# Three up projections of a fused two-block network as seven half-size products in place of eight

## The chip, the core and the metric

The kernel runs on one core of a Trainium2 chip, as one program. The metric is the device time of a run in microseconds. Its engines: TensorE (PE, matmuls; PEld is its weight load), VectorE (DVE), ScalarE (ACT), GpSimd (POOL) and SyncE (SP, which issues the weight loads).

## The reference, cut to what matters

The network has two blocks of two layers each on 512 tokens of width 1024; the first carries 256 context tokens too. All arithmetic is float32. The change lies in the feed-forwards of the second block, four in number (two in each of two layers):

```python
def rmsnorm_2(x, g, eps=EPS):
    return x * lax.rsqrt(jnp.mean(x * x, axis=-1, keepdims=True) + eps) * g

def swiglu(h, w_gate, w_up, w_down):
    return (jax.nn.silu(h @ w_gate) * (h @ w_up)) @ w_down

# second_block, layer 0 (recurrent) and 1 (attention)
x = x + 0.5 * swiglu(rmsnorm_2(x, ffn1_norm[layer]), ffn1_w_gate[layer], ffn1_w_up[layer], ffn1_w_down[layer])
h = rmsnorm_2(x, mix_norm[layer]); x = x + mixer(h)
x = x + 0.5 * swiglu(rmsnorm_2(x, ffn2_norm[layer]), ffn2_w_gate[layer], ffn2_w_up[layer], ffn2_w_down[layer])
```

The weights `w_gate` and `w_up` are 1024 x 2816, `w_down` is 2816 x 1024. So the product `h @ [w_gate, w_up]` is 512 x 1024 by 1024 x 5632.

## The kernel before, in words

Tokens lie along the free axis, width along the 128 partitions: `k.X` holds 8 tiles of 128 x 512. The width of 2816 is 22 tiles (`FT`). Each float32 operand is split into a high part (rounded to fp32r) and a low part, and a product is three matmuls, high x high, high x low, low x high (`dense`, L673 to L675).

The weights come as one stream, in the order of `split_plan`. For each chunk (128 x 1024 floats, one weight tile for all 8 width tiles): SP loads it into a ring of three raw slots, ACT writes its high part (`split_hi`, L288), DVE its low part (`split_lo`, L297), and PE uses it. There are three pairs of high and low. The split of chunk c + 2 stands in each engine's program at the step of chunk c. Each engine works through its own program in order; semaphores join them.

A feed-forward (`gated_ffn`) takes tile j of gate and of value, 24 matmuls each. DVE multiplies the gate by the root of the norm (L1304), ACT takes the SiLU (L1275), POOL multiplies by the root once more for the value (L1288), DVE multiplies by the value (L1308), and ACT and DVE split the hidden tile (L1278, L1311). The 22 tiles are cut into three groups of 8, 8 and 6; behind each group stand 8 down products over its tiles, each added to `k.X` by DVE (L1318). One tile more than the group needs is made ahead of the down products. During the last eight of them, `Feed` makes the input of what follows: ACT scales each tile of X by the gain (L903) and squares it (L906), DVE makes the low part (L914), and POOL sums the squares (L923). The root itself (L944, L949) is taken behind the first tile of the next stage. Two stages, `recurrent` and `diff_attention`, end in `ProjectOut`, which calls the same `Feed`.

The stages of the second block in order are s_up10, the recurrent mixer, s_up20, keys and values, s_up11, the attention, s_up21.

## Time and profile before

| | |
|---|---|
| Time of the runs | 3851.02, 3855.47, 3858.65 us, median 3855.47 |
| Span of the profiled execution | 3857.1 us, between the second and the third of these |
| PE busy | 3750.6 us, 97% |
| DVE, ACT, POOL busy | 51%, 35%, 10% |
| Mean granted clock of TensorE | 0.977 of 2.4 GHz |
| DMA | 330 MB, 86 GB/s |

The span is the time from the first to the last instruction of one execution; no time of that execution is given apart from it. A busy PE is not a PE at its peak, since matmuls overlap: the distance of their starts tells more than their durations. The durations of the other engines count the time in which an instruction stands still on the engine after its semaphores are there.

### The profile page before, as it was taken

How to read it: one execution, taken by the hardware profiler on the slowest of the kernel's cores; microseconds unless marked ns; L12 is line 12 of the kernel's file. 1: busy time of each engine (PE TensorE's matmuls, PEld its weight loads, DVE VectorE, ACT ScalarE, POOL GpSimd, SP SyncE). 2: the span in 40 equal slices, each digit the busy share in tenths (PEclk: the TensorE clock that was granted, in tenths of full speed). 3: DMA queues.
4: the chain of work that ended last, by engine and by line, in shares of the span. 5: the costliest groups of instructions: out<-in, count | busy, mean ns of one | idle time of the engine just before them, and what ended most of it. 6: DMA issues, size and time to landing. Idle time of an engine off the chain costs nothing.

```text
span 3857.1 us, 44920 instructions
## 1 busy us (share of the span) xinstructions
PE 3750.6 (97%) x18180; PEld 3048.8 (79%) x18180; DVE 1964.6 (51%) x3059; ACT 1334.7 (35%) x2194; POOL 390.9 (10%) x296
## 2 busy tenths in 40 slices
PE   7999999999999998999999999999999999979999
PEld 4868778888888866788888886888877888658888
DVE  5446566755546355544443457534453344574443
ACT  3245443323234334323332236322242222473222
POOL 0000002850000010000010011101020001101000
PEclk8899999999999989999999999999999999999999
DMA  5200012343322201233233332333222333203332
GB/s 214 91 28 1 1 50 81 131 134 120 121 92 76 61 28 34 87 98 98 93 99 93 98 99 82 92 97 96 93 88 88 99 98 93 67 19 97 96 97 93
DMA packets 105821, 329.99 MB, mean 86 GB/s; under 512 B 11536, under 2 KB 13200, under 8 KB 105616
## 3 DMA queue, kind: packets, MB, share of 16 engines
q1 hardware_dynamic: 103024, 320.38, 26.1%
q10 hardware_dynamic: 2592, 6.74, 0.5%
q8 instruction: 144, 2.36, 0.3%
q14 instruction: 61, 0.50, 0.0%
HBM read 324.99 MB, written 2.10 MB: 85 GB/s over the span
## 4 chain that ended last, share of the span: by engine, by line
PE 88%; DVE 3%; ACT 1%; issue 1%; POOL 0%; ACTq 0%; DVEq 0%
PE ps L673 23%; PE ps L674 23%; PE ps L675 23%; PE ps L1544 2%; PE ps L1529 1%; PE ps L1519 1%; PE ps L1520 1%; PE ps L1424 1%; PE ps L1426 1%; PE ps L1425 1%; PE ps L2637 1%; PE ps L2635 1%; PE ps L2601 1%; DVE t L3396 1%; PE ps L1516 0%
## 5 line engine op out<-in xcount | busy, mean ns | idle before, releaser
L673 PE MATMUL ps<-t 128*128 128x512 f32 (+1 forms) x4480 | 1689.0, 377 | 12.4 <-DVE t L297 9.0
L674 PE MATMUL ps<-t 128*128 128x512 f32 (+1 forms) x4480 | 1675.5, 374 | 0.0
L675 PE MATMUL ps<-t 128*128 128x512 f32 (+1 forms) x4480 | 1674.1, 374 | 0.0
L673 PEld LDWEIGHTS ps<-t 128*128 128x128 f32 x4480 | 848.9, 189 | 173.0 <-DVE t L297 10.8
L674 PEld LDWEIGHTS ps<-t 128*128 128x128 f32 x4480 | 848.9, 189 | 152.9 <-issue 5.9
L675 PEld LDWEIGHTS ps<-t 128*128 128x128 f32 x4480 | 848.3, 189 | 149.9
L297 DVE TENSOR_TENSOR t<-t 128x1024 fp32r<-128x1024 f32 (+1 forms) x517 | 645.9, 1249 | 442.4 <-ACT t L288 439.1
L288 ACT ACTIVATE t<-t 128x1024 fp32r<-128x1024 f32 (+1 forms) x517 | 533.2, 1031 | 780.0 <-PE ps L675 674.2
L1288 POOL TENSOR_TENSOR t<-t 128x512 f32<-128x512 f32 x88 | 113.8, 1293 | 1218.2 <-ACT t L1275 1218.2
L1318 DVE SCALAR_TENSOR_TENSOR t<-ps,t 128x512 f32<-128x512 f32 x96 | 66.4, 692 | 236.3 <-PE ps L675 236.3
L1278 ACT ACTIVATE t<-t 128x512 fp32r<-128x512 f32 x88 | 55.6, 632 | 340.3 <-DVE t L1308 340.3
L1275 ACT ACTIVATE t<-t 128x512 f32<-128x512 f32 x88 | 55.6, 632 | 334.9 <-DVE t L1304 334.9
L923 POOL TENSOR_TENSOR t<-t 128x512 f32<-128x512 f32 x42 | 71.0, 1690 | 769.4 <-ACT t L906 769.4
L592 DVE SCALAR_TENSOR_TENSOR t<-t 128x512 f32<-128x512 f32 x168 | 137.1, 834 | 13.6 <-DMA t<-w_ada 6.0
L1304 DVE TENSOR_TENSOR t<-ps,t 128x512 f32<-128x512 f32 x88 | 60.9, 692 | 160.5 <-PE ps L675 160.4
L1308 DVE TENSOR_TENSOR t<-ps,t 128x512 f32<-128x512 f32 x88 | 60.8, 691 | 144.8 <-PE ps L675 144.8
L1162 DVE SCALAR_TENSOR_TENSOR t<-ps,t 128x512 f32<-128x512 f32 x72 | 47.6, 662 | 127.5 <-PE ps L675 127.5
L1544 PE MATMUL ps<-t 128*128 128x64 f32 x896 | 110.7, 269 | 0.1
L1544 PEld LDWEIGHTS ps<-t 128*128 128x128 f32 x896 | 107.6, 192 | 0.2 <-ACT t L1562 0.2
L1097 ACT ACTIVATE t<-ps,t 128x512 f32<-128x512 f32 x66 | 46.1, 705 | 155.9 <-PE ps L675 149.3
L1131 DVE SCALAR_TENSOR_TENSOR t<-ps,t 128x511 f32<-128x511 f32 x66 | 43.5, 659 | 103.3 <-ACT t L1097 103.3
L1311 DVE TENSOR_TENSOR t<-t 128x512 fp32r<-128x512 f32 x88 | 61.0, 693 | 61.4 <-ACT t L1278 61.4
(381 smaller groups left out, 3461.9 us busy)
## 6 DMA issues: line engine op xcount, KB each, us to landing
t<-w_s_up SPq DMA_DIRECT2D x176, 512.0 KB, 3.6
t<-w_up SPq DMA_DIRECT2D x88, 512.0 KB, 3.7
t<-w_ada SPq DMA_DIRECT2D x160, 256.0 KB, 3.0
t<-w_s_down SPq DMA_DIRECT2D x64, 512.0 KB, 3.6
t<-w_down SPq DMA_DIRECT2D x32, 512.0 KB, 3.7
t<-w_s_down SPq DMA_DIRECT2D x32, 384.0 KB, 3.0
t<-w_ada SPq DMA_DIRECT2D x16, 512.0 KB, 10.6
t<-w_rec_in SPq DMA_DIRECT2D x16, 512.0 KB, 3.7
```

Of the source, the lines that this page charges most:

```text
L288: k.A.activation(self.hi[:, o, 0:f], self.raw[:, s, 0:f], ACT.Copy).then_inc(self.hi_done.sem, 1)
L297: k.V.tensor_tensor(self.lo[:, o, 0:f], self.raw[:, s, 0:f], self.hi[:, o, 0:f].bitcast(F32), ALU.subtract).then_inc(self.lo_done.sem, 1)
L592: ins = k.V.scalar_tensor_tensor(out=acc, in0=self.slot(h), scalar=by, in1=acc, op0=ALU.mult, op1=ALU.add)
L673: k.T.matmul(out, wh, hh, start=(i == 0), stop=False)
L674: k.T.matmul(out, wh, hl, start=False, stop=False)
L675: ins = k.T.matmul(out, wl, hh, start=False, stop=(i == len(kts) - 1))
L923: k.G.tensor_tensor(self.ACC, k.TMP[:, 0, :] if m == 1 else self.ACC, k.TMP[:, m % 2, :], ALU.add)\
L1288: k.G.tensor_tensor(a, a, RS, ALU.mult).then_inc(sm.sem, 1)
L1304: k.V.tensor_tensor(a, gate_bank[j], RS, ALU.mult).then_inc(ga.sem, 1)
L1311: k.V.tensor_tensor(lo, a, hi.bitcast(F32), ALU.subtract).then_inc(hl.sem, 1)
L1318: k.V.scalar_tensor_tensor(out=k.X[:, j, :], in0=down_bank[i], scalar=0.5, in1=k.X[:, j, :], op0=ALU.mult, op1=ALU.add).then_inc(res.sem, 1)
L1544: ins = k.T.matmul(b[:, 0:v.shape[1]], self.o(i)[:, c * 128:(c + 1) * 128], v, start=(c == 0), stop=(c == nb - 1))
```

## The change

In s_up10, s_up20 and s_up21 the up projection is done by Winograd's form of Strassen's scheme; s_up11 stays. A unit u is two tiles of gate and two of value. Its weights are four quarters: A11, A12 the gate (even and odd width tiles), A21, A22 the value. The input is cut by the parity of the width tile and by halves of the tokens, 256 each. Seven products take the place of eight: A11, S1 = A21 + A22, S2 = S1 - A11, A12, S3 = A22 - S2, S4 = A12 - S2, A22, each with one of seven blocks of the input, of which three (T2, T3, T4) and T1 are sums as well. A product is 2 x 4 x 3 = 24 matmuls of 256 columns into one of three PSUM banks.

POOL makes the four weight sums of a unit in place in the raw slots (`Stream.sum`), and all seven operands are split by ACT and DVE as chunks were. In these stages there are six raw slots and four pairs; the split stands three chunks ahead (`look`), and SP looks nine ahead. A quarter comes as two DMAs in rows of 512 bytes. `seven_ffn` puts the halves together: ACT keeps three products out of PSUM, DVE adds the later ones to them and scales, POOL scales the other two. `BlockFeed` makes the seven blocks in place of `Feed`; the recurrent and key stages have some tiles at fixed places.

```diff
...
```diff
+    def seven(up, down):
+        at = 0
+        for g, (a, b) in enumerate(GROUPS):
+            upto = min(b // 2 + 1, FT // 2)
+            order.extend((up, (u, part)) for u in range(at, upto) for part in PARTS)
+            at = upto
+            order.extend((down, 8 * g + m) for m in range(8))
...
-    feed("s_up10", "s_down10")
+    seven("s_up10", "s_down10")
...
+                if part == "A11":
+                    unit = {q: load(name, 4 * u + QUARTERS.index(q)) for q in ("A11", "A21", "A22", "A12")}
+                    self.sums[name, u] = {p: (n + PARTS.index(p), unit[q][0], unit[q][1]) for p, q in (
+                        ("A11", "A11"), ("S1", "A21"), ("S2", "A11"), ("A12", "A12"), ("S3", "A21"), ("S4", "A12"),
+                        ("A22", "A22"))}
...
+                if part in ("S3", "S4", "A22"):
+                    raw_free[x] = n
+                if part == "S4":
+                    raw_free[self.sums[name, u]["S2"][1]] = n
...
+            tiles = self.k.weights[name].rearrange("(u f g p j e n) -> u g e f p j n", f=2, g=2, p=P, j=4, e=2, n=128)
+            return [tiles[u, q // 2, q % 2, f] for f in range(2)]
...
+    def load(self, a):
         k = self.k
+        name, i, x, before, stage = self.loads[a]
+        if before >= 0:
+            if before == int(before):
+                k.sp.wait_ge(self.lo_done.at(before + 1))
+            else:
+                for t in self.opened[stage]:
+                    k.sp.wait_ge(t)
+        f = CHUNKS[name][i]
+        if name in SEVEN:
+            for h, tile in enumerate(self.source(name, i)):
+                to = self.slot(x)[:, 512 * h:512 * h + 512].rearrange("p (j n) -> p j n", j=4)
+                k.S.dma_start(to, tile).then_inc(self.landed[x].sem, 16)
+            return
...
+    def look(self, c):
+
+        for a, b in ((self.begin[x], self.finish[x]) for x in SEVEN):
+            if c < a <= c + 2:
+                return a
+            if a <= c < b:
+                return max(min(c + 3, b - 1), c + 2)
+        return c + 2
...
+
+        k, at = self.k, self.sums[name, u]
+        slot = {p: self.slot(x) for p, (n, x, t) in at.items()}
+        split = {p: self.lo_done.at(n + 1) for p, (n, x, t) in at.items()}
+        if part == "S1":
+            k.pool.wait_ge(at["S1"][2])
+            k.pool.wait_ge(at["A22"][2])
+            k.G.tensor_tensor(slot["S1"], slot["S1"], slot["A22"], ALU.add).then_inc(self.made.sem, 1)
+        elif part == "S2":
+            k.pool.wait_ge(self.made_at(name, u, "S1"))
+            k.pool.wait_ge(split["A11"])
+            k.G.tensor_tensor(slot["S2"], slot["S1"], slot["A11"], ALU.subtract).then_inc(self.made.sem, 1)
+        elif part == "S3":
+            k.pool.wait_ge(self.made_at(name, u, "S2"))
+            k.pool.wait_ge(split["S1"])
+            k.G.tensor_tensor(slot["S3"], slot["A22"], slot["S2"], ALU.subtract).then_inc(self.made.sem, 1)
+        else:
+            k.pool.wait_ge(self.made_at(name, u, "S2"))
+            k.pool.wait_ge(split["A12"])
+            k.G.tensor_tensor(slot["S4"], slot["A12"], slot["S2"], ALU.subtract).then_inc(self.made.sem, 1)
...
+class BlockFeed:
...
+    def act_hi(self, p, part):
+        k, o = self.k, self.SPANS[part]
+        if part == 0:
+            k.act.wait_ge(self.at("beside", 4 * p + 1))
+        elif part == 1:
+            k.act.wait_ge(self.at("scaled", 2 * p + 2))
+        else:
+            k.act.wait_ge(self.at("beside", 4 * p + 4) if p < 3 else self.at("late", 3))
+        k.A.activation(self.blocks.hi[:, p, o], self.Y[:, 256 + o.start:256 + o.stop], ACT.Copy).then_inc(self.sem["hi"], 1)
+
+    def act(self, m, free=()):
+        k, (p, odd) = self.k, divmod(m, 2)
+        for t in free:
+            k.act.wait_ge(t)
+        if m == 7:
+            k.stream.split_hi(self.first + 1)
+        k.act.wait_ge(self.finished(m, 0))
+        k.act.wait_ge(self.at("beside", 4 * p))
+        k.act.wait_ge(self.at("lo", 3 * p - 1 if odd else 3 * p - 2))
+        k.A.activation(self.Y[:, self.O if odd else self.E], k.X[:, m, :], ACT.Copy, scale=self.gain(m))\
+            .then_inc(self.sem["scaled"], 1)
+        if odd:
+            self.act_hi(p, 1)
+            if m == 7:
+                self.act_hi(p, 2)
+            self.act_square(m)
+        else:
+            if p:
+                self.act_hi(p - 1, 2)
+            self.act_square(m)
+            self.act_hi(p, 0)
...
+    def pool(self):
+        k, Y = self.k, self.Y
+        for p in range(4):
+            k.pool.wait_ge(self.at("scaled", 2 * p + 1))
+            k.pool.wait_ge(self.at("lo", 3 * p - 2))
+            k.pool.wait_ge(self.at("beside", 4 * p))
+            k.G.tensor_tensor(Y[:, self.T1], Y[:, 0:256], Y[:, 256:512], ALU.subtract).then_inc(self.sem["beside"], 1)
+            if p == 3:
+                k.stream.sum(self.up, 0, "S1")
+                k.stream.sum(self.up, 0, "S2")
+            self.pool_add(2 * p)
+            if p < 3:
+                k.pool.wait_ge(self.at("scaled", 2 * p + 2))
+                k.pool.wait_ge(self.at("lo", 3 * p))
+                k.pool.wait_ge(self.at("beside", 4 * p + 1))
+                k.G.tensor_tensor(Y[:, self.T2], Y[:, 768:1024], Y[:, self.T1], ALU.subtract).then_inc(self.sem["beside"], 1)
+                k.G.tensor_tensor(Y[:, self.T3], Y[:, 768:1024], Y[:, 0:256], ALU.subtract).then_inc(self.sem["beside"], 1)
+                k.pool.wait_ge(self.at("beside", 4 * p + 2))
+                k.G.tensor_tensor(Y[:, self.T4], Y[:, 1024:1280], Y[:, self.T2], ALU.subtract).then_inc(self.sem["beside"], 1)
+            self.pool_add(2 * p + 1)
...
+def seven_ffn(k, up, down, following=None):
...
+        def pe_unit(u, c):
+            for q in range(7):
+                w = st.operand(c + q, up, (u, PARTS[q]), 8)
+                if q == 0:
+                    x_bank[u], before = k.banks.take(ev.at(7 * u + 6))
+                elif q == 1:
+                    y_bank[u], before = k.banks.take(ev.at(7 * u + 4))
+                elif q == 3:
+                    z_bank[u], before = k.banks.take(ev.at(7 * u + 1))
+                elif q == 2:
+                    before = sn.at(3 * u + 1)
+                elif q == 4:
+                    before = sn.at(3 * u + 3)
+                elif q == 5:
+                    before = sn.at(3 * u + 2)
+                else:
+                    before = ev.at(7 * u + 3)
+                k.pe.wait_ge(before)
+                bank = (x_bank, y_bank, x_bank, z_bank, x_bank, y_bank, x_bank)[q][u]
+                for f in range(2):
+                    out = bank[:, 256 * f:256 * f + 256]
+                    for p in range(4):
+                        if u == 0:
+                            k.pe.wait_ge(source.ready(p, blocks[q]))
+                        bh, bl = (t[:, p, 256 * blocks[q]:256 * blocks[q] + 256] for t in (source.blocks.hi, source.blocks.lo))
+                        wh, wl = w.k(4 * f + p)
+                        k.T.matmul(out, wh, bh, start=(q in (0, 1, 3) and f == 0 and p == 0), stop=False, skip_group_check=True)
+                        k.T.matmul(out, wh, bl, start=False, stop=False, skip_group_check=True)
+                        ins = k.T.matmul(out, wl, bh, start=False, stop=(p == 3), skip_group_check=True)
+                ins.then_inc(pd.sem, 1)
+                st.used[c + q] = pd.at(7 * u + q + 1)
+                if u == 0 and q == 2:
+                    source.pe_sum()
...
+        def act_keep(u, q):
+
+            src, slot = ((x_bank, 1), (y_bank, 2), (x_bank, 0))[q]
+            k.act.wait_ge(hl.at(u - 1))
+            k.act.wait_ge(pd.at(7 * u + q + 1))
+            k.A.activation(UT[:, u % 2, slot, :], src[u], ACT.Copy).then_inc(sn.sem, 1)
+
+        def act_silu(u, h):
+            a = UT[:, u % 2, h, :]
+            k.act.wait_ge(ev.at(7 * u + (2 if h else 5)))
+            k.A.activation(a, a, ACT.Silu).then_inc(si_.sem, 1)
+
+        def act_hidden(u):
+            k.act.wait_ge(dd.at(8 * ((2 * u - HID) // 8) + 8) if 2 * u >= HID else None)
+            k.act.wait_ge(ev.at(7 * u + 7))
+            k.A.activation(hidden(hid.hi, u), UT[:, u % 2, 0:2, :].rearrange("p h (f t) -> p h f t", f=2), ACT.Copy)\
+                .then_inc(hh.sem, 1)
...
+                if kind == "up":
+                    for q in range(7):
+                        st.split_hi(st.look(c + q))
+                        if q == 0 and left is not None:
+                            act_hidden(left)
+                        if q < 3:
+                            act_keep(j, q)
+                        if j == 0 and q == 3:
+                            source.act_root()
+                        if q == 4:
+                            act_silu(j, 1)
+                        if q == 6:
+                            act_silu(j, 0)
+                    left = j
...
+        def pool_scale(u, h):
+
+            slot = 1 if h else 2
+            a = halves(UT[:, u % 2, slot, :])
+            if h:
+                k.pool.wait_ge(si_.at(2 * u + 1))
+            else:
+                k.pool.wait_ge(ev.at(7 * u + 3))
+            k.pool.wait_ge(source.rstd())
+            k.G.tensor_tensor(a, a, factor(h), ALU.mult).then_inc(rm.sem, 1)
+
+        def pool_program():
+            last = {9 // 2: 0, 17 // 2: 0, 10: 0}
+            for u in range(n_units):
+                if u in (0, 5, 9):
+                    if u:
+                        st.sum(up, u, "S1")
+                        st.sum(up, u, "S2")
+                st.sum(up, u, "S3")
+                st.sum(up, u, "S4")
+                near = u not in (4, 8, 10)
+                if near:
+                    st.sum(up, u + 1, "S1")
+                pool_scale(u, 1)
+                if near:
+                    st.sum(up, u + 1, "S2")
+                pool_scale(u, 0)
...
+        def dve_even(u, q):
+
+            t2, t1, b2 = (UT[:, u % 2, x, :] for x in range(3))
+            k.dve.wait_ge(pd.at(7 * u + q + 1))
+            if q == 3:
+                k.dve.wait_ge(sn.at(3 * u + 1))
+                k.V.tensor_tensor(t1, t1, z_bank[u], ALU.add).then_inc(ev.sem, 1)
+                k.dve.wait_ge(ev.at(7 * u + 1))
+                k.V.tensor_tensor(halves(t1), halves(t1), factor(1), ALU.mult).then_inc(ev.sem, 1)
+            elif q == 4:
+                k.dve.wait_ge(sn.at(3 * u + 2))
+                k.V.tensor_tensor(b2, b2, x_bank[u], ALU.add).then_inc(ev.sem, 1)
+            elif q == 5:
+                k.dve.wait_ge(sn.at(3 * u + 3))
+                k.V.tensor_tensor(t2, t2, y_bank[u], ALU.add).then_inc(ev.sem, 1)
+                k.dve.wait_ge(ev.at(7 * u + 4))
+                k.V.tensor_tensor(halves(t2), halves(t2), factor(0), ALU.mult).then_inc(ev.sem, 1)
+            else:
+                k.dve.wait_ge(rm.at(2 * u + 1))
+                k.V.tensor_tensor(t1, x_bank[u], t1, ALU.mult).then_inc(ev.sem, 1)
+                k.dve.wait_ge(rm.at(2 * u + 2))
+                k.dve.wait_ge(si_.at(2 * u + 2))
+                k.V.tensor_tensor(t2, t2, b2, ALU.mult).then_inc(ev.sem, 1)
+
+        def dve_hidden(u):
+            k.dve.wait_ge(hh.at(u + 1))
+            k.V.tensor_tensor(hidden(hid.lo, u), UT[:, u % 2, 0:2, :].rearrange("p h (f t) -> p h f t", f=2),
+                              hidden(hid.hi, u).bitcast(F32), ALU.subtract).then_inc(hl.sem, 1)
...
+                if kind == "up":
+                    for q in range(7):
+                        st.split_lo(st.look(c + q))
+                        if q == 0 and left is not None:
+                            dve_hidden(left)
+                        if j == 0 and q == 3:
+                            source.dve_rstd()
+                            k.dve.wait_ge(source.rstd())
+                        if q > 2:
+                            dve_even(j, q)
+                    left = j
...
-            while ahead <= min(what[1] + 2, len(st.plan) - 1):
+            while ahead < st.need[min(what[1] + (2 if what[1] < st.first_look - 3 else 9), len(st.plan) - 1)]:
...
-        half_ffn(k, "s_up10", "s_down10", following=following("mix_norm_2"))
-        recurrent(k, following("ffn2_norm_2"))
+        modulated_ffn(k, "up1", "down1", 1, False, HA, following=seven("ffn1_norm_2", "s_up10"))
+        for name in ("norm_", "gather_"):
+            k.retire(name)
+        seven_ffn(k, "s_up10", "s_down10", following=following("mix_norm_2"))
```
```

POOL's program in the first changed stage, before: the sums of squares (L923) and the 22 multiplications by the root (L1288), and what stands around them (L2699 in the first block's mixer, L2937 in the recurrent one).

```order
L2699 TENSOR_TENSOR t<-t 128x128 x40
L923 TENSOR_TENSOR t<-t 128x512 x7
L1288 TENSOR_TENSOR t<-t 128x512 x22
L923 TENSOR_TENSOR t<-t 128x512 x7
L2937 TENSOR_TENSOR t<-t 128x512 x8
```

The same engine after, from the second unit of s_up10 on. L436, L440, L444 and L448 make S1, S2, S3 and S4, L1783 scales; `raw_more` are the three slots more.

```order
L1783 TENSOR_TENSOR t<-t 128x512
L440 TENSOR_TENSOR raw_more_49<-raw_more_49 128x1024
L1783 TENSOR_TENSOR t<-t 128x512
L444 TENSOR_TENSOR raw_more_49<-t,raw_more_49 128x1024
L448 TENSOR_TENSOR raw_more_49<-raw_more_49 128x1024
L436 TENSOR_TENSOR t<-t,raw_more_49 128x1024
L1783 TENSOR_TENSOR t<-t 128x512
L440 TENSOR_TENSOR t<-t 128x1024
```

A row of POOL's between two SiLUs has become a queue in which the scaling (L1783) stands behind the next unit's S1, and the next S3 behind both scalings.

DVE before, for one tile: the splits (L297), the gate (L1304), the value (L1308) and the hidden tile's low part (L1311).

```order
L1304 TENSOR_TENSOR t<-ps,t 128x512
L297 TENSOR_TENSOR t<-t 128x1024
L1308 TENSOR_TENSOR t<-ps,t 128x512
L1311 TENSOR_TENSOR t<-t 128x512
L297 TENSOR_TENSOR t<-t 128x1024
```

DVE after, for one unit, from the split of A12 to the last but one step. L421 is the split, L1830 the hidden tile of the unit before, L1810 to L1826 put the products together; the rows with `ps` read PSUM.

```order
L421 TENSOR_TENSOR t<-t 128x1024
L1830 TENSOR_TENSOR t<-t 128x2x2x256
L421 TENSOR_TENSOR t<-t 128x1024
L421 TENSOR_TENSOR lo_more_51<-t,hi_more_50 128x1024
L421 TENSOR_TENSOR t<-raw_more_49,t 128x1024
L1810 TENSOR_TENSOR t<-t,ps 128x512
L1812 TENSOR_TENSOR t<-t 128x512
L421 TENSOR_TENSOR t<-raw_more_49,t 128x1024
L1815 TENSOR_TENSOR t<-t,ps 128x512
L421 TENSOR_TENSOR t<-t 128x1024
L1818 TENSOR_TENSOR t<-t,ps 128x512
L1820 TENSOR_TENSOR t<-t 128x512
```

The split of S2, L1823 and L1826 follow. For two tiles DVE had four splits and six operations of 512 columns; now it has seven splits, one of 1024 for the hidden tiles and seven of 512.

## Rows read from the trace of the kernel before

**Rows 1.** The page: section 1, and the chain that ended last (section 4)
```profile
span 3857.1 us, 44920 instructions
...
PE 3750.6 (97%) x18180; PEld 3048.8 (79%) x18180; DVE 1964.6 (51%) x3059; ACT 1334.7 (35%) x2194; POOL 390.9 (10%) x296
...
PE 88%; DVE 3%; ACT 1%; issue 1%; POOL 0%; ACTq 0%; DVEq 0%
PE ps L673 23%; PE ps L674 23%; PE ps L675 23%; PE ps L1544 2%; PE ps L1529 1%; PE ps L1519 1%; PE ps L1520 1%; PE ps L1424 1%; PE ps L1426 1%; PE ps L1425 1%; PE ps L2637 1%; PE ps L2635 1%; PE ps L2601 1%; DVE t L3396 1%; PE ps L1516 0%
```

**Rows 2.** 100 us of s_up10: busy us of each engine (x instructions), clock, DMA
```profile
2000.00:2100.00 100.00, 100.00 (x443) 82.81 (x442) 39.58 (x43) 24.31 (x28) 6.46 (x5) 1.00 0.32 96
```

**Rows 3.** Timeline of PE where the width changes: start us, us, line, form
```profile
805.13 0.28 PE L673 MATMUL ps<-t 128*128 128x256 f32 x1
...
807.89 0.28 PE L675 MATMUL ps<-t 128*128 128x256 f32 x1
808.01 0.40 PE L673 MATMUL ps<-t 128*128 128x512 f32 x1
```

**Rows 4.** Single lines: count, duration in ns as min/median/max, forms
```profile
L297 DVE TENSOR_TENSOR t<-t x517: 953/1226/1733, 52.6 to 3843.0; 128x1024 fp32r<-128x1024 f32 x156, 128x768 fp32r<-128x768 f32 x17
...
L288 ACT ACTIVATE t<-t x517: 829/1044/1101, 46.7 to 3842.1; 128x1024 fp32r<-128x1024 f32 x156, 128x768 fp32r<-128x768 f32 x17
...
L1308 DVE TENSOR_TENSOR t<-ps,t x88: 677/692/692, 1949.7 to 3821.7; 128x512 f32<-128x512 f32 x88
...
L1097 ACT ACTIVATE t<-ps,t x66: 549/777/782, 648.8 to 1897.5; 128x512 f32<-128x512 f32 x44, 128x256 f32<-128x256 f32 x22
...
L1288 POOL TENSOR_TENSOR t<-t x88: 1289/1292/1298, 1947.4 to 3817.7; 128x512 f32<-128x512 f32 x88
...
L2699 POOL TENSOR_TENSOR t<-t x40: 395/398/1377, 1354.8 to 1455.9; 128x128 f32<-128x128 f32 x40
```

**Rows 5.** Timeline of DVE and POOL at two places in it
```profile
1912.90 0.75 DVE L914 SCALAR_TENSOR_TENSOR t<-t 128x512 fp32r<-128x512 f32 x1
...
1913.21 1.58 POOL L923 TENSOR_TENSOR t<-t 128x512 f32<-128x512 f32 x1 [456.90 <-ACT t L906]
...
1947.41 1.30 POOL L1288 TENSOR_TENSOR t<-t 128x512 f32<-128x512 f32 x1 [8.32 <-ACT t L1275]
...
1948.31 1.47 DVE L297 TENSOR_TENSOR t<-t 128x1024 fp32r<-128x1024 f32 x1 [1.65 <-ACT t L288]
```

**Rows 6.** Timeline of the same two near 652 us
```profile
651.62 1.57 POOL L612 TENSOR_SCALAR t<-t 128x512 f32<-128x512 f32 x1 [25.97 <-DVE t L592]
...
652.15 0.75 DVE L1134 SCALAR_TENSOR_TENSOR t<-ps,t 128x511 f32<-128x511 f32 x1
```

**Rows 7.** SP's waits; then DMA issues: count, KB each, median us to landing
```profile
SPq L278 <- DVE t L297: 2610.4, 439, 110.9
...
t<-w_s_up SPq DMA_DIRECT2D x176, 512.0 KB, 3.6
...
t<-xT SPq DMA_DIRECT2D x1, 2048.0 KB, 18.3
...
t<-consts ACTq DMA_DIRECT2D x2, 64.0 KB, 3.4
```

**Rows 8.** The reciprocal of a root, and the table loads, as in group 4
```profile
L949 DVE RECIPROCAL t<-t x5: 3345/3352/3353, 1942.6 to 3501.4; 128x512 f32<-128x512 f32 x5
...
L1275 ACT ACT_TABLE_LOAD  x4: 1283/1283/1283, 1942.6 to 3501.4; - x4
```

**Rows 9.** PE around a stop: timeline, then its windows
```profile
2410.97 0.77 PE L673 MATMUL ps<-t 128*128 128x512 f32 x1 [2.68 <-DVE t L3039]
...
2412.39 0.63 PE L673 MATMUL ps<-t 128*128 128x512 f32 x1
2412.82 0.63 PE L674 MATMUL ps<-t 128*128 128x512 f32 x1
...
2412.00:2414.00 2.00, 2.00 (x6) 0.50 0.03 8
```

351 lines of the change are left out of this document (303 added, 48 removed).

## The prediction

> **What bounds the kernel now.** I read the page from the top down. TensorE is busy for 97% of the span, and the chain that ended last is 88% PE, 70% of it on the three matmul lines L673, L674 and L675 [rows 1]. Then I took 100 us inside s_up10, one of the three stages that change. PE has no gap there, the granted clock is 1.00 (2.4 GHz), and the others have room: DVE 40, ACT 24 and POOL 6 us [rows 2]. So time comes off only if PE gets less to do, and only as long as the engines with room keep up with it. Those are the two questions.
>
> **TensorE's part.** What matters is the distance between matmul starts, not the 390 ns that one is given. Of 128x512, 443 lie in 100 us: 0.2257 us each [rows 2]. Of 128x256, 24 lie between 805.13 and 808.01 us: 0.120 us each [rows 3], so half the columns cost 53%, with a weight load for each. Two tiles of gate and value took 4 x 24 = 96 wide matmuls, 96 x 0.2257 = 21.67 us. A unit of the new stage does the same with 7 products of 24 narrow ones, 168 x 0.120 = 20.16 us (2.88 a product). That is 1.51 us less, and 33 units (11 in each of three stages) give 49.8 us. The down products stay.
>
> **What is added beside it, per unit.** The durations are from [rows 4]. POOL: four sums of 1024 columns and two scalings of 512. One of 512 takes 1.29 us and one of 128 takes 0.40, 2.33 ns a column, so 1024 cost 2.48 us: 4 x 2.48 + 2 x 1.29 = 12.5 us. DVE: seven low splits and one low part of the hidden tile, each 1.23 us, and seven operations on 512 columns of 0.69: 14.7 us. ACT: seven high splits and the hidden tile at 1.04, and three copies out of PSUM and two SiLUs at 0.78 or less (L1097): 12.2 us at most. Each fits in 20.16 us. Before, two tiles cost DVE 9.0 us and POOL 2.6.
>
> **The two together don't fit.** At 1947.41 POOL starts a two-input operation of 1.30 us. DVE's split starts 0.90 later and takes 1.47 instead of 1.23: they lie side by side for 0.40 us, and DVE loses 0.24. At 1912.90 DVE is first with 0.75 us; POOL starts 0.31 later and takes 1.58 instead of 1.29, with 0.44 side by side [rows 5, 4]. The one that comes second stands still until about 0.15 us before the other's end; it isn't slowed in proportion, it waits. A DVE operation with one input in PSUM doesn't: L1134 keeps its 0.75 us beside POOL's L612 [rows 6]. The Trainium skill says so too (SBUF — State Buffer, "Who interferes with whom": a VectorE instruction with two SBUF inputs and a GpSimd instruction that reads SBUF exclude each other); the traces agree with it, and by it as by the rows the operations must be added, not laid side by side.
>
> So I add what needs the shared port, taking 0.15 off each: POOL 4 x 2.33 + 2 x 1.14 = 11.6 us. On DVE 8 x 1.08 + 3 x 0.54 = 10.3 us (the splits, the hidden tile, two scalings by the root, the product of the halves). Together 21.9 us per unit, over the 20.16 of PE and over the 21.67 of before. With nothing overlapping at all, PSUM operations included, it is 14.7 + 12.5 = 27.2 us. These are the ends. To choose I wrote one steady unit out, POOL and DVE taking turns. Three things come on top of the floor: the add from PSUM after the fourth product (0.65), which nothing of POOL's covers, since POOL then waits for the SiLU that follows from it; some 14 handovers at 0.05 us (0.7); and the next S1, which needs quarter A22. That one is loaded into the slot that the split of S3 frees, 4.5 us later (3.6 to land [rows 7] and the issues); POOL idles through about 0.8 us that DVE can't fill. That makes 24.0 us per unit.
>
> **How it reaches TensorE.** The third product adds to the bank of the first, so it waits for ACT's copy of that. On ACT the copy is queued behind the hidden tile of the unit before, which waits for DVE's last product (L1826 of the changed kernel), which waits for POOL's second scaling. Hence PE stops once a unit, ahead of its third product, for 24.0 - 20.2 = 3.8 us. Three products are split ahead, which gives a lead of some 5 us, so the first unit behind a group of down products is free and the second stops for 1 us. Groups have 5, 4 and 2 units, that is 3 + 2 + 0 full stops a stage and 15 in all: 57 us. The short ones of groups two and three: 6 x 1 = 6 us. The last hidden tile of a stage is needed at once by the down products, and it now comes after two port operations: 1 us each, 3 us.
>
> **The entry of a stage.** Before, the root of the norm cost PE nothing: the reciprocal (3.35 us) and the two table loads (1.28 each) lay beside PE, since the gate's bank could wait [rows 8]. Now three things meet. Sums S1 and S2 of the first unit stand in POOL's queue among the block sums, and ACT's split of S1 stands ahead of the last tile's scaling, so blocks T2 to T4 and the split of S2 are ready about 8.5 us after the last down product, where the third product wants them at 5.8: 2.7 us. The root then puts 3.35 us of DVE and a table load in front of the first SiLU, with only two sets of hidden tiles, so that the second unit stops for about 6 us. Some 8.5 us a stage, 25 us in all; the ends are 0 (all of it in the lead) and 13 a stage (each delay in full).
>
> **Costed at nothing.** The 512-byte rows of the quarter loads: the queue waited 2,610 us for free slots, so it has room [rows 7], and a load of 64 KB in rows of 512 bytes took 3.4 us. Nearest from above is 4.6 us per 512 KB (xT, 2 MB in 18.3). If a quarter lands 3 us later than I assume, POOL's S1 comes later and each steady unit costs about 2 us more, 30 us in all. The moved tiles of the recurrent and key stages keep their waits. More matmuls mean more instructions, all fetched beside the work.
>
> **Sum**, against the profiled execution, whose span is 3857.1 us (the timed runs lie from 3851.0 to 3858.7 about a median of 3855.5, so both stand for the same time): 3857.1 - 49.8 + 57 + 6 + 3 + 25 = 3898.3 us. Against the median, 1.6 less: 3897 us.
>
> **Rivals.**
> *PE stays the bound.* If the exclusion falls where one of the two has slack anyway, PE gives its 49.8 us and loses only some entry: 3857 - 50 + 5 = 3812 us. For it: each engine alone has over 5 us of room per unit. Against it: 21.9 us of port in 20.16. It would need the port's time to be under 92% of what [rows 5] give. Chance 0.12. This is the case that ends faster.
> *The port is filled without gaps.* A unit takes 21.9, and groups start with a lead and end with a lighter unit (no sums for a next one, 4.7 us less). Then a group is held up by 0 to 3 us: about 5 us a stage, and half the entry cost: 3857 - 50 + 15 + 20 = 3842, up to 3860 with the entry in full. POOL waiting for the SiLU is against it. Chance 0.20, half of it faster, half within the measurement.
> *The stops are dearer.* PE stops for 2.7 us ahead of 2410.97. After it the granted clock is 0.50, half of 2.4 GHz, and the next six to seven matmuls start 0.43 us apart rather than 0.226: 1.5 us lost [rows 9]. Stops of 3.8 us are longer. Fifteen with 1.5 us each make 22 us: 3920. With late quarters as well 3950. Speaking against it, a lower clock is partly covered, since the port, not PE, closes the cycle. Chance 0.20.
> The forecast itself has 0.48. That the change doesn't do what it says has no chance worth a number; the order of the instructions shows it.
>
> **Numbers.** What a measurement of this kernel can tell from no change is 0.2%, or 7.7 us. Faster: 0.12 + 0.10 = 0.22. Same: 0.10. Slower: 0.68. The range goes from the middle of the second rival's low side, 3825, to 3945, which leaves out about 0.1 on each side. The forecast's own range is 3870 to 3920.
>
> **What would show it.** PE's time without stops: narrow matmuls 0.120 us apart, 20.2 us of work a unit. If they stand further apart, the first term is wrong. Steady units 24 us apart, with one stop each on ACT's copy out of PSUM (L1732 of the changed kernel); units of 20.2 would sink the forecast. POOL's sums longer than 2.48 us in the mean, DVE's splits longer than 1.23, and the excess of the two together 3 us or more a unit: without it the exclusion isn't what counts. POOL with S1 waiting for a DMA would show late quarters. A PEclk under 0.95 in the changed stages would show the third rival. The feed-forward s_up11, left as it is, has to stay within 1 us of its time.

## The result, and the profile after

The changed kernel takes 3924.24 us (median of four runs, 3920.96 to 3927.62) against 3855.45 (3851.02 to 3858.65) for the kernel before: a ratio of 1.0181, 95% interval 1.0166 to 1.0195. It is slower by 69 us. The forecast was 3897 us, 27 too low, with "slower" at 0.68.

From the page of the changed kernel: span, busy time, granted clock by slice, chain [rows 1].

```profile
span 3922.7 us, 50614 instructions
...
PE 3727.8 (95%) x20556; PEld 3137.0 (80%) x20556; DVE 2327.2 (59%) x3245; ACT 1508.9 (38%) x2395; POOL 857.4 (22%) x467
...
PEclk8999999999999989999999999999999999999999
...
PE 74%; DVE 8%; ACT 4%; issue 3%; POOL 3%; DMA 1%; SPq 0%; DVEq 0%; ACTq 0%; POOLq 0%
```

PE has more instructions and is busy for less time than before, and its share of the chain has fallen from 88% to 74%. What it lost stands mostly with DVE (8%, from 3), ACT (4%, from 1) and POOL (3%, from 0): TensorE has less to do, and waits for the engines that feed it.

What PE waited for in the changed stages (us in total, times, longest):

```profile
PE ps L1704 <- ACT t L1732: 57.5, 26, 3.9
...
PE ps L1704 <- DVE t L1815: 13.5, 3, 4.9
PE ps L1704 <- DVE t L421: 10.4, 6, 3.1
...
PE ps L1704 <- DVE blocks_lo L1173: 3.1, 1, 3.1
PE ps L822 <- DVE t L1830: 3.0, 3, 1.0
```

In the three stages themselves the kernel before had no wait at all. L1732 is ACT's copy of a product out of PSUM. Of its 57.5 us, 6.1 (5 waits) lie in the first two units of a stage; the other 51.4 (21 waits) are the steady and short stops that the prediction spoke of. L1815 is the add behind which the seventh product of a stage's first unit waits; the root of the norm stands ahead of it on DVE.

I then cut the program at the starts of its matmuls. The columns are the window, its length, busy us (x instructions) of PE, PEld, DVE, ACT and POOL, granted clock, DMA share and GB/s, as in [rows 2]. The kernel before makes 9, 8 and 5 tiles of gate and value ahead of its three rounds of down products, the changed one 5, 4 and 2 units, that is 10, 8 and 4 tiles. So the first two windows of before are cut to the work of five and of four units; they run a little way into the down products, whose matmuls have the same width and spacing. Before: these two, then keys and values, then s_up11 with its down products.

```profile
1935.40:2044.70 109.30, 109.30 (x482) 90.14 (x481) 51.12 (x51) 35.00 (x43) 13.32 (x11) 1.00 0.32 99
2088.20:2175.20 87.00, 87.00 (x386) 72.03 (x385) 37.93 (x40) 24.79 (x31) 9.05 (x7) 1.00 0.32 101
2873.90:2930.30 56.40, 56.40 (x219) 39.58 (x218) 21.61 (x22) 16.22 (x20) 2.62 (x2) 1.00 0.26 83
2930.30:3347.10 416.80, 416.80 (x1855) 342.80 (x1855) 176.99 (x201) 122.64 (x155) 47.65 (x35) 1.00 0.31 95
```

After: the same four stretches.

```profile
1932.29:2063.35 131.06, 110.19 (x843) 107.83 (x842) 115.83 (x83) 62.44 (x76) 84.80 (x34) 0.92 0.33 100
2106.90:2196.16 89.26, 82.54 (x674) 82.01 (x673) 75.06 (x58) 42.33 (x51) 55.00 (x21) 0.96 0.34 104
2912.10:2972.60 60.50, 60.50 (x219) 41.68 (x218) 21.60 (x22) 16.23 (x20) 2.58 (x2) 0.94 0.23 78
2972.60:3391.20 418.60, 418.60 (x1855) 342.85 (x1855) 176.98 (x201) 122.65 (x155) 47.73 (x35) 1.00 0.29 95
```

The work of the second group, four units, took 87.0 us and takes 89.3. That of the first, five units, took 109.3 and takes 131.1, at a clock of 0.92. A stretch at half clock counts 0.5, so 0.92 means that some 16% of that window ran at 1.2 GHz.

Over all nine groups of the three stages, each from its first matmul to the first one behind it: 720.8 us before, 778.4 after. The rest of the span: 3136.3 before, 3144.3 after. In the changed kernel's groups the distances between matmul starts fall into three kinds: 0.118 us (full clock); 0.15 to 0.7 us, which exceed 0.118 by 34.7 us in all; and stops, 91.0 us in all. The middle kind is called half clock below: nearly all of it lies where the granted clock is 0.50, a small part (2.9 us in the kernel with narrow sums below) is very short stops.

### The profile page after: what moved, and what is told of

It is laid out like the page before. It is cut to its first block, busy times and chain, and to the rows that moved or that the text cites. A ratio compares the mean times of both kernels' runs of the same rounds, so it can differ in the third digit from the quotient of the medians.

```text
span 3922.7 us, 50614 instructions
## 1 busy us (share of the span) xinstructions
PE 3727.8 (95%) x20556; PEld 3137.0 (80%) x20556; DVE 2327.2 (59%) x3245; ACT 1508.9 (38%) x2395; POOL 857.4 (22%) x467
## 4 chain that ended last, share of the span: by engine, by line
PE 74%; DVE 8%; ACT 4%; issue 3%; POOL 3%; DMA 1%; SPq 0%; DVEq 0%; ACTq 0%; POOLq 0%
PE ps L822 17%; PE ps L824 16%; PE ps L823 16%; PE ps L2089 2%; PE ps L1704 2%; PE ps L1706 2%; PE ps L1705 2%; PE ps L2074 1%; DVE t L1826 1%; PE ps L2064 1%; POOL raw_more L440 1%; DVE t L421 1%; PE ps L2065 1%; PE ps L1969 1%; PE ps L1970 1%
## 5 line engine op out<-in xcount | busy, mean ns | idle before, releaser
L822 PE MATMUL ps<-t 128*128 128x512 f32 (+1 forms) x2620 | 956.4, 365 | 6.9 <-DVE t L1830 3.0
L823 PE MATMUL ps<-t 128*128 128x512 f32 (+1 forms) x2620 | 949.8, 363 | 0.0
L824 PE MATMUL ps<-t 128*128 128x512 f32 (+1 forms) x2620 | 949.0, 362 | 0.0
L421 DVE TENSOR_TENSOR t<-t 128x1024 fp32r<-128x1024 f32 (+1 forms) x433 | 587.7, 1358 | 341.9 <-ACT t L408 338.6
L822 PEld LDWEIGHTS ps<-t 128*128 128x128 f32 x2620 | 498.1, 190 | 91.3 <-issue 6.7
L823 PEld LDWEIGHTS ps<-t 128*128 128x128 f32 x2620 | 498.0, 190 | 77.4 <-issue 1.9
L824 PEld LDWEIGHTS ps<-t 128*128 128x128 f32 x2620 | 497.6, 190 | 76.9
L1704 PE MATMUL ps<-blocks_hi,t 128*128 128x256 f32 x1392 | 400.9, 288 | 65.8 <-ACT t L1732 38.9
L1705 PE MATMUL ps<-blocks_lo,t 128*128 128x256 f32 x1392 | 397.1, 285 | 0.0
L1706 PE MATMUL ps<-blocks_hi,t 128*128 128x256 f32 x1392 | 396.4, 285 | 0.0
L1704 PEld LDWEIGHTS ps<-blocks_hi,t 128*128 128x128 f32 x1392 | 270.5, 194 | 71.5 <-DVE t L421 36.7
L822 PE MATMUL ps<-tail_hi,t 128*128 128x512 f32 x672 | 270.6, 403 | 8.0 <-DVE t L421 8.0
L1705 PEld LDWEIGHTS ps<-blocks_lo,t 128*128 128x128 f32 x1392 | 270.2, 194 | 0.1
L1706 PEld LDWEIGHTS ps<-blocks_hi,t 128*128 128x128 f32 x1392 | 270.0, 194 | 0.0
L824 PE MATMUL ps<-tail_hi,t 128*128 128x512 f32 x672 | 263.7, 392 | 0.0
L823 PE MATMUL ps<-tail_lo,t 128*128 128x512 f32 x672 | 262.6, 391 | 0.0
L408 ACT ACTIVATE t<-raw_more 128x1024 fp32r<-128x1024 f32 (+1 forms) x108 | 111.7, 1034 | 192.7 <-PE ps L824 82.3
L421 DVE TENSOR_TENSOR t<-raw_more,t 128x1024 fp32r<-128x1024 f32 (+1 forms) x108 | 152.4, 1411 | 38.1 <-ACT t L408 37.7
L822 PEld LDWEIGHTS ps<-tail_hi,t 128*128 128x128 f32 x672 | 126.7, 189 | 38.1 <-DVE t L421 8.8
L1859 DVE SCALAR_TENSOR_TENSOR t<-ps,t 128x512 f32<-128x512 f32 x72 | 49.8, 691 | 179.4 <-PE ps L824 179.4
L1704 PE MATMUL ps<-blocks_hi,hi_more 128*128 128x256 f32 x456 | 134.9, 296 | 18.7 <-ACT t L1732 18.7
```

Source lines behind the costliest of these rows:

```text
L408: k.A.activation(self.pair(n)[0], self.slot(self.raw_at[n])[:, 0:self.size(n)], ACT.Copy)\
L421: k.V.tensor_tensor(lo, self.slot(self.raw_at[n])[:, 0:self.size(n)], hi.bitcast(F32), ALU.subtract).then_inc(self.lo_done.sem, 1)
L822: k.T.matmul(out, wh, hh, start=(i == 0), stop=False)
L823: k.T.matmul(out, wh, hl, start=False, stop=False)
L824: ins = k.T.matmul(out, wl, hh, start=False, stop=(i == len(kts) - 1))
L1704: k.T.matmul(out, wh, bh, start=(q in (0, 1, 3) and f == 0 and p == 0), stop=False, skip_group_check=True)
```

## A steady stop, row by row

The timeline of the changed kernel of s_up10 around the stop ahead of the third product of its fourth unit (start us, us, engine, line):

```profile
2018.25 3.38 POOL L444 TENSOR_TENSOR t<-t,raw_more 128x1024 f32<-128x1024 f32 x1
...
2019.89 2.29 DVE L1826 TENSOR_TENSOR t<-t 128x512 f32<-128x512 f32 x1
...
2021.26 0.28 PE L1706 MATMUL ps<-blocks_hi,t 128*128 128x256 f32 x1
...
2022.21 1.06 ACT L1742 ACTIVATE t<-t 128x1024 fp32r<-128x1024 f32 x1 [3.07 <-DVE t L1826]
2023.17 0.58 ACT L1732 ACTIVATE t<-ps 128x512 f32<-128x512 f32 x1
...
2023.90 0.55 PE L1704 MATMUL ps<-blocks_hi,hi_more 128*128 128x256 f32 x1 [2.36 <-ACT t L1732]
...
2024.24 0.41 PE L1705 MATMUL ps<-blocks_lo,hi_more 128*128 128x256 f32 x1
...
2026.98 0.28 PE L1706 MATMUL ps<-blocks_hi,lo_more 128*128 128x256 f32 x1
```

Read it from the top. POOL makes S3 (L444), 3.38 us, where the shortest sum of the run takes 2.39. DVE's last product of the unit (L1826) starts beside it at 2019.89 and ends at 2022.18, half a microsecond after POOL: 2.29 us for what takes 0.69 alone. ACT's hidden tile (L1742) follows at once and behind it the copy (L1732). PE has run dry at 2021.5 and has been idle for 2.36 us when the third product starts at 2023.90. Then come a dozen matmuls 0.21 us apart, and at 2026.98 those 0.12 apart begin. So a stop has two prices: its length, and a tail at half clock.

By form, in the second group (line, form, count | busy, mean ns), DVE first, then POOL:

```profile
L421 DVE TENSOR_TENSOR t<-t 128x1024 fp32r<-128x1024 f32 x12 | 18.7, 1560 | 7.0 <-ACT t L408 6.9
...
L1820 DVE TENSOR_TENSOR t<-t 128x512 f32<-128x512 f32 x4 | 7.3, 1836 | 0.1
L1826 DVE TENSOR_TENSOR t<-t 128x512 f32<-128x512 f32 x3 | 6.8, 2282 | 0.0
```
```profile
L1783 POOL TENSOR_TENSOR t<-t 128x512 f32<-128x512 f32 x8 | 13.5, 1687 | 8.5 <-ACT t L1737 8.5
L448 POOL TENSOR_TENSOR t<-t,raw_more 128x1024 f32<-128x1024 f32 x4 | 12.6, 3145 | 13.7 <-DVE t L421 11.9 <-DVE lo_more L421 1.8
```

L1820 and L1826 take 0.69 us where nothing is in the way, here 1.84 and 2.28; the 512-column scaling of POOL 1.69 in place of 1.29 [rows 4], and its 1024-column sums 3.15 (L448).

The entry of s_up10, DVE and then POOL:

```profile
1932.65 3.93 DVE L1173 TENSOR_TENSOR blocks_lo<-t,blocks_hi 128x768 fp32r<-128x768 f32 x2 [2.21 <-ACT blocks_hi L1146]
1936.51 0.74 DVE L1455 SCALAR_TENSOR_TENSOR t<-ps,t 128x512 f32<-128x512 f32 x1
1937.17 2.76 DVE L421 TENSOR_TENSOR t<-t 128x1024 fp32r<-128x1024 f32 x1
1939.85 1.50 DVE L1186 TENSOR_TENSOR t<-t 128x256 f32<-128x256 f32 x1
```
```profile
1932.98 3.06 POOL L436 TENSOR_TENSOR t<-t 128x1024 f32<-128x1024 f32 x1
1936.11 2.73 POOL L440 TENSOR_TENSOR t<-t 128x1024 f32<-128x1024 f32 x1
```

The low parts of two blocks (L1173, two instructions) take 3.93 us, since POOL's S1 (L436) lies beside the second. The last tile's residual (L1455), from which the last scaling and so T2 to T4 follow, comes only at 1936.51, and the next split and T2 stand behind S2 (L440) in turn.

## The experiments

All ratios are to the kernel before, run beside each on the same chip, with 95% intervals. "Groups" is the sum over the nine groups of the three stages (720.8 us before, 778.4 in the changed kernel).

### Rows of the quarter loads, and the sums almost taken away

The first experiment reads each quarter in rows of 2 KB; the weights that arrive are then others:

```diff
-            for h, tile in enumerate(self.source(name, i)):
+            o = self.offset[name][i]
+            for h in range(2):
+                tile = k.weights[name][o + 65536 * h:o + 65536 * h + 65536].rearrange("(p j n) -> p j n", p=P, j=4)
```

> The quarter loads of the changed kernel in rows of 2 KB instead of 512 bytes (same two DMAs and bytes, the weights land in another order, so the products are of other numbers). Theory (DVE and POOL exclude each other on the shared port): the loads are a side matter, POOL's S1 starts a little earlier, 3910 to 3924 us, and the splits keep their mean of about 1.4 us. Rival (late quarters): POOL waited 215 us for DMAs ahead of S1 in all; if that sets the units, 25 us or more come off, 3895 us or less.

Measured: 3920.40 us, 1.0165 (1.0150 to 1.0181). PE's waits in it:

```profile
PE ps L1706 <- ACT t L1734: 48.3, 25, 2.6
...
PE ps L1706 <- DVE t L1817: 19.1, 12, 4.7
```

The stops are all there (and 11.7 us behind splits). Late quarters are at most a small part here: the time is inside the first range. The groups take 774.3 us, 4 less, but the interval overlaps that of the changed kernel, so no gain is shown.

The second lets POOL sum 64 of the 1024 columns, all instructions and waits kept (S1 shown, the others alike):

```diff
-            k.G.tensor_tensor(slot["S1"], slot["S1"], slot["A22"], ALU.add).then_inc(self.made.sem, 1)
+            k.G.tensor_tensor(slot["S1"][:, 0:64], slot["S1"][:, 0:64], slot["A22"][:, 0:64], ALU.add).then_inc(self.made.sem, 1)
```

> The four weight sums only over the first 64 of 1024 columns, every wait as in the changed kernel. Theory: POOL's hold of the port falls from 11.6 to about 3 us a unit, the steady stops of TensorE go, what stays is the entry of a stage with the root: 3857 - 60 (narrow matmuls at 0.118 us) + 8 a stage = 3820 us, 3810 to 3835. Rival (the chain of waits itself stops PE: three copies out of PSUM, two sets of hidden tiles): more than half of the 2.5 us stops stay, 3865 us or more.

Measured: 3813.53 us, 0.9894 (0.9877 to 0.9910), faster than the kernel before. First and second group of s_up10:

```profile
1934.94:2040.84 105.90, 100.85 (x843) 99.57 (x842) 85.25 (x83) 63.72 (x76) 32.66 (x34) 1.00 0.41 124
2084.40:2163.55 79.15, 79.15 (x674) 79.15 (x673) 58.70 (x58) 43.79 (x51) 19.32 (x21) 1.00 0.38 118
```

Groups: 664.4 us. Behind the entry there is no stop and no half clock in any of the three stages, so the chain of waits by itself doesn't stop PE. Four units take 79.15 us, 672 matmuls at 0.1178. DVE works off the same 58 instructions in 58.70 us in place of 75.06: 4.1 us less a unit. All that the change lost is in the sums of POOL and in what they do to the others.

### Long on POOL, or reading beside DVE?

A sum is slow for PE either because POOL takes 2.4 us for it, or because it and DVE exclude each other. Here each sum is replaced by three fills of the same slot, which write 1024 columns each and read nothing:

```diff
+    def fill(self, slot):
+        k = self.k
+        for _ in range(2):
+            k.G.memset(slot, 0.5).then_inc(self.pad.sem, 1)
+            self.pads += 1
+            k.pool.wait_ge(self.pad.at(self.pads))
+        return k.G.memset(slot, 0.5)
...
-            k.G.tensor_tensor(slot["S1"], slot["S1"], slot["A22"], ALU.add).then_inc(self.made.sem, 1)
+            self.fill(slot["S1"]).then_inc(self.made.sem, 1)
```

> Each weight sum is replaced by three fills of its slot with a constant, with all its waits: POOL stays busy for some 2.5 us a sum and reads nothing. Theory: the splits on DVE fall back to 1.23 us in the mean, because a fill needs no read port, and most of the stops go: 3825 to 3850 us. Rival (POOL is simply too slow and late in its queue, the port is beside the point): the stops stay as they are, 3900 us or more.

Measured: 3820.00 us, 0.9910 (0.9895 to 0.9925), 5 us under the range that I expected. DVE's splits in the second group, then POOL's fills and the split beside them:

```profile
L422 DVE TENSOR_TENSOR t<-t 128x1024 fp32r<-128x1024 f32 x12 | 15.5, 1295 | 9.6 <-ACT t L409 9.6
```
```profile
2122.20 1.96 POOL L432 MEMSET t<- 128x1024 f32 x2 [5.12 <-DMA t<-w_s_up]
2124.22 0.95 POOL L435 MEMSET t<- 128x1024 f32 x1
```
```profile
2123.52 1.22 DVE L422 TENSOR_TENSOR t<-raw_more,t 128x1024 fp32r<-128x1024 f32 x1
```

POOL is kept busy for 2.97 us by each "sum", longer than by the real one, and at 2123.52 DVE's split runs in 1.22 us beside two fills. The four-unit groups take 79.15 us again. So behind the entry the length of POOL's work costs TensorE nothing; what costs is that a GpSimd instruction with two inputs in SBUF and a DVE one of the same kind stand still for each other. The Trainium skill (SBUF — State Buffer, "Who interferes with whom") ties the exclusion to GpSimd reading SBUF; the fills bear that out. At the entry it is otherwise: there stops and half clock come to 25.4 us with the fills and 14.0 with the narrow sums, though this profiled execution is also 9 us above its kernel's median.

### The sums on DVE

If the port has to be shared in any case, the faster engine should do the work. DVE makes the sums here but S1 and S2 of units 0, 5 and 9:

```diff
+                        if q == 0:
+                            if j in (0, 5, 9):
+                                st.sum(up, j, "S3", True)
+                            st.sum(up, j, "S4", True)
...
+                        if 2 < q < 6 and j not in (4, 8, 10):
+                            st.sum(up, j + 1, PARTS[(1, 2, 4)[q - 3]], True)
```

> The sums go to DVE but for S1 and S2 of the first unit of each group; S3, S4 stand behind the split that frees their slot, S1, S2 of the next unit behind the fourth and fifth product. Same arithmetic. Theory: DVE gets 4 x 1.14 us more, 18.0 of 20.2 us a unit, POOL keeps the two scalings, the port's sum is 10.3 + 4.3 + 2.3 = 16.9 us, so no steady stop; the entry stays: 3825 to 3850 us, faster than before. Rival (DVE in its fixed order becomes the bound): stops of 1 to 2 us a unit, 3865 to 3890 us.

Measured: 3870.71 us, 1.0041 (1.0028 to 1.0054): 54 us better than the changed kernel, but 21 above the upper end of what I expected, and inside what the rival (DVE in its fixed order becomes the bound) gave. A sum takes 1.22 us on DVE against 2.39 to 3.4 on POOL. PE's waits, then the second group:

```profile
PE ps L1707 <- ACT t L1735: 22.6, 21, 1.3
...
PE ps L1707 <- DVE t L1810: 14.7, 10, 3.8
```
```profile
2093.45:2176.94 83.49, 79.75 (x674) 78.80 (x672) 76.90 (x72) 42.89 (x51) 14.38 (x8) 1.00 0.36 112
```

A stop of 1.2 us a unit is left on the copy, and DVE is busy for 76.90 of 83.49 us. With so little room its order counts: S3 of the next unit stands ahead of the product of the halves, for which the hidden tile and the copy wait. So S3 goes one place back:

```diff
-                        if 2 < q < 6 and j not in (4, 8, 10):
-                            st.sum(up, j + 1, PARTS[(1, 2, 4)[q - 3]], True)
+                        if q in (3, 4, 6) and j not in (4, 8, 10):
+                            st.sum(up, j + 1, {3: "S1", 4: "S2", 6: "S3"}[q], True)
```

> The kernel with the sums on DVE (3870.7 us, with a stop of 1.2 us a unit ahead of the third product), and in it S3 of the next unit moved on DVE from behind the sixth product to behind the seventh. If DVE's order is what makes that stop (S3 stands ahead of the product of the halves, which ACT's hidden tile and behind it the copy out of PSUM wait for), the product of the halves comes 1.1 to 1.2 us sooner and the steady stops go: 20 to 25 us off, 3845 to 3851 us, the first group's units 20.2 to 20.6 us apart. If the stop is DVE's total load or what is left of the exclusion with POOL's scalings, the order doesn't matter: 3866 to 3875. The entry's 10 us stay.

Measured: 3859.48 us, 1.0017 (1.0007 to 1.0026), 11 us better where I expected 20 to 25. The stops on the copy are gone, and others of 1.0 to 1.3 us stand in some units, ahead of a product that waits for DVE's add from PSUM:

```profile
PE ps L1707 <- DVE t L1810: 24.9, 16, 4.7
```

### The entry, with the sums on POOL and on DVE

The entry's edit: S1 and S2 of the first unit on DVE, the last tile's square ahead of its last high split, and the root one product earlier. In the core:

```diff
             self.dve_lo(p, 0)
+            if m == 6:
+                k.stream.sum(self.up, 0, "S1", True)
+                k.stream.sum(self.up, 0, "S2", True)
...
-            if p == 3:
-                k.stream.sum(self.up, 0, "S1")
-                k.stream.sum(self.up, 0, "S2")
...
-                if u == 0 and q == 2:
+                if u == 0 and q == 1:
                     source.pe_sum()
```

On the changed kernel:

> The changed kernel with its entry alone rewritten: the first unit's S1 and S2 of each stage on DVE instead of in POOL's queue, and the root of the norm one product earlier. If the entry costs what the trace of the changed kernel shows in its first 42 us (13.5 us of stops and some 6 us of half clock over three stages, where 25 were forecast), at most 20 us can come back; DVE gets two more two-input operations of 1.21 us a stage, so I expect 10 to 17 us back: 3907 to 3914 us. If the forecast's reading were right that POOL's queue and the root are the whole of the entry (8.5 us a stage), 20 to 25 us: 3900 to 3904. If the entry is bound by the last tile's own chain and not by these two, no difference: 3920 to 3926. The steady stops of 2.5 to 4 us a unit stay in all three.

Measured: 3917.83 us, 1.0174 (1.0159 to 1.0189), between my first range and the last, and not told apart from the changed kernel. DVE at the entry, where 3.93 us stood above:

```profile
1927.70 2.86 DVE L1176 TENSOR_TENSOR blocks_lo<-t,blocks_hi 128x768 fp32r<-128x768 f32 x2 [2.21 <-ACT blocks_hi L1149]
1930.48 1.21 DVE L439 TENSOR_TENSOR t<-t 128x1024 f32<-128x1024 f32 x1
```

The pair of low parts is down to 2.86 us, two sums of 1.21 and 1.23 us have come in front of the residual instead. The first two units have 39.1 us of stops and half clock over the three stages in place of 48.7; the later ones 82.3 in place of 77.0. The stop ahead of the first unit's seventh product, which stood behind the root (13.9 us over the three stages), is gone; those ahead of its first five are not (20.0 us, 19.2 before), and the second unit's grew from 3.1 to 7.6. More than half of what the entry gave back was lost behind it.

On the kernel with the sums on DVE and S3 moved back:

> The kernel before this one, and the entry rewritten too: the first unit's S1 and S2 on DVE ahead of the last tile's step, the square of the last tile ahead of its last high split, and the root of the norm behind the second product. POOL then makes sums only for the first units behind the down products of groups one and two. If the entry's stops come from those two sums in POOL's queue and from the root standing in front of the first SiLU, 10 to 15 us more come off: 3830 to 3840 us, faster than the kernel before (3855) by 0.4 to 0.6%. If the entry is bound by the last tile's own chain, nothing comes off: 3845 to 3851.

Measured: 3852.74 us, 1.0001 (0.9992 to 1.0010), 7 us less where 10 to 15 were expected (the two intervals just touch); the groups give 8.0 us (714.0 to 706.0). The timeline of DVE in a unit of the second group shows what is left, and POOL's scaling beside it:

```profile
2128.75 2.33 DVE L439 TENSOR_TENSOR t<-t 128x1024 f32<-128x1024 f32 x1 [0.79 <-DMA t<-w_s_up]
2131.00 1.21 DVE L421 TENSOR_TENSOR t<-raw_more,t 128x1024 fp32r<-128x1024 f32 x1
2132.14 0.67 DVE L1810 TENSOR_TENSOR t<-t,ps 128x512 f32<-128x512 f32 x1
```
```profile
2128.71 1.29 POOL L1786 TENSOR_TENSOR t<-t 128x512 f32<-128x512 f32 x1 [14.88 <-ACT t L1740]
```

DVE stands for 0.79 us for a quarter; S1 then falls beside POOL's scaling and takes 2.33 us in place of 1.22; split and add from PSUM (L1810) come late. With the sums on DVE a late quarter can cost what it didn't before, so the loads were tried again, one transfer of 4 KB rows a quarter, with the data laid out for it:

```diff
-            return [tiles[u, q // 2, q % 2, f] for f in range(2)]
+            o = (4 * u + q) * P * SLOT
+            return self.k.weights[name][o:o + P * SLOT].rearrange("(p f) -> p f", p=P)
...
-            for h, tile in enumerate(self.source(name, i)):
-                to = self.slot(x)[:, 512 * h:512 * h + 512].rearrange("p (j n) -> p j n", j=4)
-                k.S.dma_start(to, tile).then_inc(self.landed[x].sem, 16)
-            return
```

> The kernel before this one with each quarter of the up weights as one transfer of 128 rows of 4 KB instead of two with 512-byte rows; its data are laid out for it beforehand. Where the port no longer holds back POOL or DVE, a late quarter would show as a wait of S1 for a DMA. If loads are off the path: the same time within 3 us. If the rows cost (the same edit took 0 to 8 us off the changed kernel): 4 to 8 us less. The bound from TensorE alone, 3857.1 less 49.8, is 3807 us.

Measured: 3842.84 us, 0.9977 (0.9968 to 0.9987). Its second group:

```profile
2088.78:2168.93 80.15, 79.03 (x674) 78.27 (x672) 75.83 (x72) 43.25 (x51) 15.08 (x8) 1.00 0.33 114
```

This version beats both kernels: 81 us under the changed one, 10.6 (0.1 to 0.3%) under the one before. The second group's stops fell from 2.3 to 0.8 us. With POOL making the sums, two transfers of 2 KB rows had given 4 us at most; this edit goes further, and which part of it counts, the longer rows or the single transfer, was not tried.

### The price of a stop, and of the entry

The forecast gave each steady stop its length alone. To price one away from the port, the kernel with sums over 64 columns got 15 stops made by ACT, which repeats a copy out of PSUM:

```diff
+            if q == 0 and u in (2, 3, 4, 7, 8):
+                for _ in range(7):
+                    k.A.activation(UT[:, u % 2, slot, :], src[u], ACT.Copy).then_inc(st.pad.sem, 1)
+                    st.pads += 1
+                    k.act.wait_ge(st.pad.at(st.pads))
```

> The kernel with sums over 64 columns (3813.5 us, no stops behind the entry), and in it ACT repeats the copy of the first product out of PSUM seven more times in units 2, 3, 4, 7 and 8 of each stage: 15 stops of TensorE of 3 to 4.3 us that have nothing to do with the port, at the places where the forecast put its full stops. It prices a stop with all that follows on the clock. If a stop costs only its length, the groups grow by 45 to 64 us and the half-clock time stays at 2.9 us: 3859 to 3878. If each brings 1.5 us of half clock as in the kernel before (rival 3 of the prediction): 22 us more, 3881 to 3900. If only some 0.9, as in the groups of four units of the changed kernel (2.7 us over three stops): 3873 to 3891.

Measured: 3873.09 us, 1.0049 (1.0032 to 1.0065). The second group, and the stops:

```profile
2098.31:2184.30 85.99, 81.14 (x673) 80.79 (x672) 58.03 (x58) 51.96 (x65) 19.21 (x21) 0.98 0.36 109
```
```profile
PE ps L1705 <- ACT t L1738: 36.3, 15, 2.4
```

Fifteen stops of 2.4 us waited (each 2.6 beyond the usual distance of matmul starts) are followed by 14.8 us at half clock in all, though nothing on the port had changed. In the mean a stop with its tail costs 3.6 us, 1.4 times its length. The groups grow by 57.7 us; the other 4 lie at the entries and in one first group. The time fits the first of the three ranges as well as the third; the half clock decides against the first.

The mean hides two kinds. The fifteen stops are alike, but the first of each group (units 2 and 7, six in all) has no tail, and the nine that follow one unit later lose 1.6 us each. Three microseconds from the start of the third product in units 7 and 8:

```profile
2146.12:2149.12 3.00, 3.00 (x25) 3.00 (x26) 1.95 (x2) 2.24 (x3) 0.00 (x0) 1.00 0.00 0
2168.57:2171.57 3.00, 3.00 (x15) 3.00 (x16) 1.96 (x2) 2.23 (x3) 0.00 (x0) 0.55 0.00 0
```

Behind the first the granted clock stays at 1.00 (2.4 GHz), behind the second it is down to 0.55 on average, mostly at 1.2 GHz. In unit 7 PE had run without a stop since the down products, in unit 8 it had stopped a unit before. The changed kernel has the same two kinds behind its 21 stops past the entry: nine of 1.8 to 1.9 us have no tail, the nine in the first groups (2.5 to 3.9 us) lose 1.4 to 1.6 us each, and the longest of each second group (3.5 to 4.0 us) loses 2.5 to 2.8. That makes 22.2 us.

The entry alone, with the four sums of each stage's first unit at full width and the others over 64 columns:

```diff
+        w = 64 if u else 1024
...
-            k.G.tensor_tensor(slot["S1"][:, 0:64], slot["S1"][:, 0:64], slot["A22"][:, 0:64], ALU.add).then_inc(self.made.sem, 1)
+            k.G.tensor_tensor(slot["S1"][:, 0:w], slot["S1"][:, 0:w], slot["A22"][:, 0:w], ALU.add).then_inc(self.made.sem, 1)
```

> The kernel with sums over 64 columns (3813.5 us), but with the four sums of the first unit of each stage at full width, so that only the entry of the changed kernel is there. If the entry's stops (11 to 16 us a stage in the first 42 us of the changed kernel) and its half clock (6 us a stage) come from the first unit's sums alone, the groups grow by about 40 us over three stages: 3850 to 3857. If they are the sums of the second unit, queued right behind, that hold it back (S1, S2 for unit 1 stand on the port in the same stretch), less than half of it: 3820 to 3833. With the exclusion irrelevant there, nothing: 3811 to 3817.

Measured: 3837.46 us, 0.9955 (0.9940 to 0.9970): 24 us more than with no full sum, between my two figures. Its first group; the second has no stop:

```profile
1930.90:2046.42 115.52, 105.25 (x843) 103.72 (x842) 90.53 (x83) 63.96 (x76) 42.81 (x34) 0.96 0.37 113
```

So the entry has three parts. In stops and half clock of the first two units: 14.0 us with no full sums at all (7.2 ahead of the first three products, 4.0 ahead of the seventh, behind the root, the rest short distances), 24.2 more with the first unit's sums, and 10.5 that are left for the sums of the units behind it; that last part is a difference, no run shows it alone. Together 48.7 us.

## Why the prediction came out as it did

The terms, in us. The measured column is of the two profiled executions; behind it how it is made.

| Term | Forecast | Measured |
|---|---|---|
| TensorE's products | -49.8 | -68.1 (720.8 to 778.4 - 91.0 - 34.7) |
| Steady and short stops | +63 | +77.0 (21 stops, 54.8, and 22.2 at half clock) |
| Entry | +25 | +48.7 (36.2 of stops, 12.5 at half clock) |
| Last hidden tile | +3 | +3.0 (L822 behind L1830) |
| Rest of the program | 0 | +5.0 |
| Sum | +41.2 | +65.6 |

*What failed* is the term "the entry of a stage". It was given 8.5 us a stage with ends of 0 and 13, and cost 16.2. Of its two delays the prediction had one about right: it gave the root and the second unit 6 us a stage, and the stops ahead of the first unit's seventh product (behind the root, 4.6) and in the second unit (1.0) make 5.7. The other it had wrong: 2.7 us a stage ahead of the third product, where the first five products have 6.4. It counted there that S1 and S2 stand in POOL's queue and that ACT's split of S1 stands ahead of the last scaling; no delay on the port appears in it, though splits, block sums and weight sums hold each other up there while the last tile is still being made. And it gave the half clock of the entry nothing; that is 4.2 us a stage. The experiments show that 24 of the 48.7 us come with the first unit's sums at full width, and that 14 are there with none. They also show that it isn't a matter of POOL's queue: with S1 and S2 on DVE the stops ahead of the first five products were all there. The exclusion isn't separated from the rest of the entry as cleanly as from the steady stops: with fills in place of the sums, which read nothing, the entry still costs 25.4 us.

*Off in both directions* are two terms that belong together. A matmul of 256 columns comes 0.1178 us apart, not 0.120, and 512 columns take 0.2267 (384 in 87.0 us), not 0.2257: the 443 rows in 100 us include those that reach in over the window's edge. That makes the products 18 us better than forecast. The stops past the entry, with their half clock, are 14 us worse. But the prediction itself says that in a steady unit the port closes the cycle, so what PE gains there it waits longer. Steady units of the first groups stand 23.8 to 25.2 us apart, 24.3 in the mean of the nine, and are made of 19.8 us of matmuls, 3.0 of stop and 1.5 of half clock, where 20.2, 3.8 and 0 were forecast. The two terms together missed by 4 us, to the good side (8.9 for 13.2), and the steady cycle was sized well. The groups of four units, 89.3 to 89.5 us against 4 x 20.16 + 2 x 3.8 + 1 = 89.2, agree in the same way, with all three parts different: that closeness is partly luck.

*The clock.* The prediction's own sign for the rival "the stops are dearer", a clock under 0.95 in the changed stages, is there in the first groups of s_up10 and s_up20 (0.92 each), but not in that of s_up21 (0.95) or in any second group (0.96). Its mechanism is real: the ACT-made stops show tails of 1.6 us away from the port. But where the port closes the cycle, the sums above speak for a covered tail, as the prediction argued: the 1.5 us a steady stop that the rival adds are not in the unit's length. No run tests that by itself. That its 3920 us lies nearer to 3924 than the forecast does is mostly luck, since what is missing from the forecast came at the entry. The outcome lies above the forecast's own range (3870 to 3920) and inside the whole one.

*Right, by its own signs.* The steady stop sits on L1732, once a unit, ahead of the third product, behind DVE's L1826 and POOL. The lengths differ from the plan: twelve stops of 2.5 to 4.0 us and nine of 1.8 to 1.9, where fifteen of 3.8 and six of 1 stood. Steady units come 24.3 us apart against 24.0. DVE's and POOL's operations carry an excess, DVE alone 4.1 us a unit against the kernel with narrow sums. And the exclusion on reading stood the test against the rival "POOL is just slow".

*The rivals.* "PE stays the bound" would give 3812 us; with the sums cut to 64 columns it is 3813.5. Its condition wasn't met in the changed kernel, and that its sum agrees is luck: the profiled execution has 70.4 us off for the products, 14.0 added at the entry and 12.0 in the rest of the program, where 50, 5 and 0 stood. "The port is filled without gaps" (21.9 us a unit) is shown by no run. With the sums on DVE units of the first groups take 21.0 to 22.1 us behind the entry, but there DVE itself is nearly full (76.90 of 83.49 us in the second group). Late quarters were worth 4 us of the groups at most.

*Small misses.* s_up11 takes 418.6 us, not 416.8, so it didn't stay within 1 us; keys and values take 60.5 in place of 56.4, at a clock of 0.94 where 1.00 stood, without a wait that differs. In all the kernels with narrow products the stretch from s_up20 to s_up21 is 5 to 12 us longer, 9.4 in the changed one. Why the clock falls there was not settled. Against it stand 3.1 us less ahead of s_up10, a stretch that differs by up to 11 us between the profiled executions of these kernels, so that a miss of a few microseconds in the rest of the program can't be read.

## What to carry to other kernels

Before moving work to an idle engine, add up what it and its neighbour need of what they share, and not only each engine's busy time; here 12.5 and 14.7 us fitted into 20 by themselves and didn't together. A matrix engine that stops pays the stop and often a tail: here all twelve stops of 2.5 us and over in the changed kernel, past the entry, and nine of fifteen alike ones made by ACT lost 1.4 us or more at half clock, and the shorter ones nothing. Where another engine closes the cycle, the tail takes the place of waiting. The entry of a stage, where all engines are busy with what comes before, has to be counted by itself. And the same sums on the engine that is twice as fast at them, in the right order and with the loads widened, turned a loss of 69 us into a gain of 11.

## What the runs showed of the hardware

- Fills by POOL don't exclude DVE (splits of 1.22 us beside them). Of 1024 columns each takes 0.95 us, a sum of two inputs 2.39, the same on DVE 1.22.
- What is left of POOL's work still costs: with sums over 64 columns DVE's splits in the second group take 1.39 us in the mean, not 1.22, beside two scalings a unit.
- L1810 and L1823 on DVE, which read PSUM, have a median of 0.69 and 0.68 us over all 33 units, beside POOL or not.
- Of fifteen alike stops of 2.6 us that ACT made, the first of each group leaves the granted clock at 1.00, and the next ones are followed by 1.6 us lost at half clock each. In the changed kernel one of 2.4 us is followed by a dozen matmuls 0.21 us apart, and nine of 1.8 to 1.9 us by none.
